# Up-projections of the gated MLPs as seven block products a tile, all seven low parts of its weights on GpSimd

## What is computed

```python
def conv_ffn(h, w_up, conv_w, conv_b, w_down):
    gate, val = jnp.split(h @ w_up, 2, axis=-1)
    gate = lax.conv_general_dilated(
        gate, conv_w[:, None, :], window_strides=(1,), padding=((CONV_WIDTH - 1, 0),),
        dimension_numbers=('NWC', 'WIO', 'NWC'), feature_group_count=D_FF) + conv_b
    return (jax.nn.silu(gate) * val) @ w_down

x = x + conv_ffn(rms_norm(x, ffn_norm_g[layer]), ...)      # D_FF = 2816, D_MODEL = 1024
```

## Time and profile before

| | |
|---|---|
| median of 3 runs | 1221.3 us |
| span of the profiled execution | 1219.5 us |
| up-projections in it, tiles 1 to 21 of a layer | 228.5 us, twice |
| down-projections in it, nine tiles of each | 97.9 us, twice |
| TensorE, VectorE, ScalarE, GpSimd busy | 1207.9, 507.8, 501.6, 567.4 us |
| granted TensorE clock, mean | 0.999 |

### The profile page before, as it was taken

The page is one execution under the profiler, slowest core; times in us unless marked ns, Lnnn a source line. Parts: engine busy times, 40 slices in busy tenths (PEclk is TensorE's granted clock), DMA queues, the critical chain, the costliest instruction groups (busy, mean ns, idle before and its releaser), DMA issues.

```text
span 1219.5 us, 16989 instructions
## 1 busy us (share of the span) xinstructions
PE 1207.9 (99%) x6230; PEld 1036.3 (85%) x6230; DVE 507.8 (42%) x900; ACT 501.6 (41%) x743; POOL 567.4 (47%) x509
## 2 busy tenths in 40 slices
PE   8999999999999999999999999999999999999997
PEld 7999999888888888888888889888888888888886
DVE  7878777653211212323241375635321212232325
ACT  6665555544322223423342366344332322343234
POOL 2435544335444444566645332613544444456662
PEclk9999999999999999999999999999999999999999
DMA  7222222113222222222223211301322222222221
GB/s 270 92 98 95 79 70 70 67 38 121 103 103 103 73 99 103 104 84 89 104 87 121 87 70 57 117 36 39 123 98 103 103 92 86 97 103 104 75 98 70
DMA packets 17325, 113.71 MB, mean 93 GB/s; under 512 B 1920, under 2 KB 2304, under 8 KB 4608
## 3 DMA queue, kind: packets, MB, share of 16 engines
q1 hardware_dynamic: 16416, 110.20, 25.2%
q10 hardware_dynamic: 864, 2.88, 0.7%
HBM read 110.98 MB, written 2.10 MB: 93 GB/s over the span
## 4 chain that ended last, share of the span: by engine, by line
PE 95%; DVE 2%; ACT 1%; issue 1%; DMA 0%; DVEq 0%; SPq 0%; ACTq 0%
PE ps L1600 38%; PE ps L1893 16%; PE ps L1681 9%; PE ps L1543 7%; PE ps L1572 3%; PE ps L2024 2%; PE ps L1722 2%; PE ps L1645 2%; PE ps L2004 2%; PE ps L1590 2%; PE ps L1650 1%; PE ps L1928 1%; PE ps L1708 1%; PE ps L1491 1%; PE ps L1734 1%
## 5 line engine op out<-in xcount | busy, mean ns | idle before, releaser
L316 POOL TENSOR_TENSOR w_lo<-w_raw,w_hi 128x512 fp32r<-128x512 f32 (+1 forms) x329 | 462.5, 1437 | 515.5 <-ACT w_hi L413 459.5
L413 ACT ACTIVATE w_hi<-w_raw 128x2048 fp32r<-128x2048 f32 (+1 forms) x93 | 171.9, 1848 | 309.1 <-PE ps L1600 155.2
L1600 PE MATMUL ps<-hT_hi,w_hi 128*128 128x512 f32 x688 | 267.7, 389 | 0.0
L1600 PE MATMUL ps<-hT_hi,w_lo 128*128 128x512 f32 x688 | 267.7, 389 | 0.0
L1600 PE MATMUL ps<-hT_lo,w_hi 128*128 128x512 f32 x688 | 267.6, 389 | 0.0
L1600 PEld LDWEIGHTS ps<-hT_hi,w_hi 128*128 128x128 f32 x688 | 129.1, 188 | 26.8
L1600 PEld LDWEIGHTS ps<-hT_lo,w_hi 128*128 128x128 f32 x688 | 129.1, 188 | 26.8
L1600 PEld LDWEIGHTS ps<-hT_hi,w_lo 128*128 128x128 f32 x688 | 129.1, 188 | 26.7
L1235 DVE TENSOR_TENSOR hT_lo<-region,hT_hi 128x2048 fp32r<-128x2048 f32 (+1 forms) x22 | 58.9, 2684 | 144.0 <-ACT hT_hi L686 144.0
L1205 DVE SCALAR_TENSOR_TENSOR qk<-ps,vec,qk 128x511 f32<-128x511 f32 x44 | 33.0, 750 | 200.1 <-ACT qk L660 200.1
L660 ACT ACTIVATE qk<-ps,vec 128x512 f32<-128x512 f32 x44 | 34.3, 780 | 175.5 <-PE ps L1600 166.3
(11 more groups left out here) (278 smaller groups left out, 2102.3 us busy)
## 6 DMA issues: line engine op xcount, KB each, us to landing
w_raw<-weights SPq DMA_DIRECT2D x99, 1024.0 KB, 4.8
gain<-gains ACTq DMA_DIRECT2D x4, 512.0 KB, 3.5
x<-x_in SPq DMA_DIRECT2D x3, 512.0 KB, 7.5
out<-region SPq DMA_DIRECT2D x3, 512.0 KB, 2.7
w_raw<-weights SPq DMA_DIRECT2D x2, 384.0 KB, 5.6
w_raw<-weights SPq DMA_DIRECT2D x1, 768.0 KB, 8.6
cst<-consts SPq DMA_DIRECT2D x1, 640.0 KB, 10.2
x<-x_in ACTq DMA_DIRECT2D x1, 512.0 KB, 4.1
```

What stands on the lines that cost most here:

```text
L316: ins = pool.tensor_tensor(w_lo[:, slot, cols], w_raw[:, slot, cols], w_hi[:, slot, cols].bitcast(f32), ALU.subtract)
L413: sc.activation(w_hi[:, slot, 0:used], w_raw[:, slot, 0:used], ACT.Copy).then_inc(w_hi_ready, 1)
L1600: ins = pe.matmul(bank, w[:, slot, k * pitch + 128 * s:k * pitch + 128 * s + 128], h[:, k:k + 1, :], start=k == 0 and n == 0, stop=k == KT ...
```

## The change

In both MLPs, up tiles 2 to 21 are no longer multiplied as 2 x 2 blocks in the plain way (eight block products) but as seven block products by Winograd's form of Strassen's scheme. The weights of a tile are four blocks A11, A12, A21, A22 (128 output channels by 512 inputs), the activations four blocks B11 to B22 (512 inputs by 256 tokens).

- **Weights.** VectorE makes S1 = A21 + A22, S2 = S1 - A11, S3 = A11 - A21 and S4 = A12 - S2 for each tile, 512 columns each (`block_sums`). ScalarE makes high parts of A11, A12, A22 in one instruction of 1536 columns, of S1 in one of 512, of S2 to S4 in one of 1536. GpSimd makes the seven low parts, 512 columns each (`block_lows`), where it made four.
- **Activations.** Once a layer, ScalarE copies the turned activations from PSUM to SBUF (`copy_raw`, eight instructions), and VectorE makes T1 to T4 and, with ScalarE, their two parts. T3 takes the place of B12.
- **Products.** Seven for each tile, each 4 input blocks x 3 products of 256 columns: 84 of 256 columns a tile (`block_tile`), in the order 1, 2, 3, 5, 6, 4, 7. Gate tiles use PSUM banks 0 to 3, value tiles 4 to 7.
- **Combining.** ScalarE copies product 1 to SBUF (`copy_p1`), VectorE combines the seven products in four instructions into `z` in SBUF (`combine_block`). The convolution's steps and the multiply by the SiLU read `z` instead of PSUM.
- **Edges.** The first two tiles of a layer are multiplied as before, in other banks. The first down tile reads `hT_hi`, `hT_lo` instead of `first_hi`, `first_lo`. `load_gain` moves from before the MLP to behind it.

```diff
+        T_PLACES = ((xn_at, xn_at + 4096), (xn_at + 8192, cst_at + 4 * C_CMUL), (act_end, act_end + 4096))
+        t_hi = [at(f"t_hi{j}", [128, 4, 256], a) for j, (a, b) in enumerate(T_PLACES)]
+        t_lo = [at(f"t_lo{j}", [128, 4, 256], b) for j, (a, b) in enumerate(T_PLACES)]
+        t_raw = [at(f"t_raw{j}", [128, 4, 256], b, f32) for j, (a, b) in enumerate(T_PLACES)]
+        z = region[:, 13312:15104]
+        p1 = (region[:, 15104:15360], vec[:, 0:256])
+        S_PLACES = ((region_at + 4 * 15360, late_at), (late_at + 4 * 1536, spare_at))
+        s_hi = [at(f"s_hi{j}", [128, 1536], a) for j, (a, b) in enumerate(S_PLACES)]
+        s_lo = [at(f"s_lo{j}", [128, 1536], b) for j, (a, b) in enumerate(S_PLACES)]
+        s_raw = [at(f"s_raw{j}", [128, 1536], b, f32) for j, (a, b) in enumerate(S_PLACES)]
+        s1_raw = [at(f"s1_raw{j}", [128, 512], w_lo_at + 4 * (UNIT * j + 1536), f32) for j in range(2)]
+        raw_h = region[:, 14 * SEQ:FT * SEQ].rearrange("p (j n) -> p j n", j=KT)
+        t3_raw = region[:, 12 * SEQ:14 * SEQ].rearrange("p (k n) -> p k n", k=4)
+        z1, z2 = z[:, 512:1024], z[:, 0:512]
...
+            def block_lows(l, n0):
+
+                with pool.Fori(1, PAIRS) as i:
+                    for half in range(2):
+                        tile = 2 * i + (half - 2)
+                        pool.wait_ge(w_hi_ready, 2 * i + (n0 + half + 1))
+                        for a in (0, 512):
+                            low(w_lo[:, half, a:a + 512], w_raw[:, half, a:a + 512], w_hi[:, half, a:a + 512])
+                        pool.wait_ge(s_summed[l], tile + 1)
+                        low(w_lo[:, half, 1024:1536], w_raw[:, half, 1024:1536], w_hi[:, half, 1024:1536])\
+                          .then_inc(w_lo_ready, 1)
+                        pool.wait_ge(s_high[l], 2 * tile + 1)
+                        low(w_lo[:, half, 1536:UNIT], s1_raw[half][:, :], w_hi[:, half, 1536:UNIT]).then_inc(s_low[l], 1)
+                        pool.wait_ge(s_high[l], 2 * tile + 2)
+                        for a, made in ((1024, s4_low[l]), (0, s_low[l]), (512, s_low[l])):
+                            low(s_lo[half][:, a:a + 512], s_raw[half][:, a:a + 512], s_hi[half][:, a:a + 512])\
+                              .then_inc(made, 1)
+
             pool.wait_ge(w_lo_ready, W_OUT0 + 1)
-            split_range(W_OUT0 + 1, W_C + 2)
+            split_range(W_OUT0 + 1, W_UP0 + 2)
+            block_lows(0, W_UP0)
+            split_range(W_DN0, W_C + 2)
...
+            def copy_raw(l, t, before):
+
+                for g in range(2):
+                    sc.wait_ge(turn_lo, 8 * before + 2 * t + g + 1)
+                    sc.activation(raw_h[:, 4 * g:4 * g + 4, t * 128:(t + 1) * 128],
+                                  ps[:, MLP_TURN[t] + g, :].rearrange("p (j n) -> p j n", j=4), ACT.Copy)\
+                      .then_inc(raw_copied[l], 1)
...
+                before_mlp = k in (1, 3)
+                if before_mlp:
+                    copy_raw(k // 2, 0, turns[0])
...
+                if before_mlp:
+                    for t in (2, 1, 3):
+                        copy_raw(k // 2, t, turns[0] - 1)
...
+                def block_high(i, half):
+
+                    sc.wait_ge(mm_done, 8 * i + 4 * (n0 + half - 1))
+                    sc.wait_ge(w_loaded[half], 16 * i + 16 * (n0 // 2 + 1))
+                    sc.activation(w_hi[:, half, 0:1536], w_raw[:, half, 0:1536], ACT.Copy).then_inc(w_hi_ready, 1)
+
+                def sum_highs(i, half):
+
+                    sc.wait_ge(s_summed[l], 2 * i + (half - 1))
+                    sc.activation(w_hi[:, half, 1536:UNIT], s1_raw[half][:, :], ACT.Copy).then_inc(s_high[l], 1)
+                    sc.activation(s_hi[half][:, :], s_raw[half][:, :], ACT.Copy).then_inc(s_high[l], 1)
+
+                def copy_p1(i, half):
+
+                    sc.wait_ge(product_done[l], 4 * i + (2 * half - 3))
+                    sc.activation(p1[half], ps[:, 4 * half + 3, 0:256], ACT.Copy).then_inc(p1_copied[l], 1)
...
+                    sc.wait_ge(act_done[l], 2)
+                    sc.wait_ge(product_done[l], 4 * LAST)
...
+                def pair(i, last=False):
+                    block_high(i, 1)
+                    copy_p1(i, 0)
+                    sum_highs(i, 1)
+                    if last:
+                        split_after(n1 - 2)
+                    else:
+                        block_high(i + 1, 0)
+                    copy_p1(i, 1)
+                    if not last:
+                        sum_highs(i + 1, 0)
+                    sc.wait_ge(combined[l], 2 * i + 1)
+                    for s in range(2):
+                        gate_start(i, s, (z1, z2)[s])
+                    silu(i)
...
+                for j, summed in enumerate((1, 3, 4)):
+                    sc.wait_ge(t_summed[l], summed)
+                    sc.activation(t_hi[j][:, :, :], t_raw[j][:, :, :], ACT.Copy).then_inc(t_high[l], 1)
+                for s in range(2):
+                    sc.wait_ge(mm_done, 4 * n0 + 2 * s + 2)
+                    gate_start(0, s, ps[:, 6 + s, :])
+                block_high(1, 0)
+                sum_highs(1, 0)
+                silu(0)
+                sc.wait_ge(t_summed[l], 4)
+                sc.wait_ge(mm_done, 4 * (n0 + 2))
+                sc.activation(hT_hi[:, 0:4, 256:512], t3_raw, ACT.Copy).then_inc(t_high[l], 1)
...
+                def block_sums(i, half):
+
+                    a11, a12, a22, a21 = (w_raw[:, half, 512 * j:512 * j + 512] for j in range(4))
+                    s1, (s2, s3, s4) = s1_raw[half][:, :], (s_raw[half][:, 512 * j:512 * j + 512] for j in range(3))
+                    ve.wait_ge(mm_done, 8 * i + 4 * (n0 + half - 1))
+                    ve.wait_ge(w_loaded[half], 16 * i + 16 * (n0 // 2 + 1))
+                    first = own.mark(ve.tensor_tensor(s1, a21, a22, ALU.add))
+                    ve.tensor_tensor(s3, a11, a21, ALU.subtract)
+                    own.wait(first)
+                    own.link(ve.tensor_tensor(s2, s1, a11, ALU.subtract))
+                    ve.tensor_tensor(s4, a12, s2, ALU.subtract).then_inc(s_summed[l], 1)
+
...
+                def combine_block(i, half, last=False):
+
+                    b = 4 * half
+                    if not last:
+                        ve.wait_ge(product_done[l], 4 * i + (2 * half - 2))
+                    else:
+                        ve.wait_ge(mm_done, 4 * n1)
+                    ve.wait_ge(p1_copied[l], 2 * i + (half - 1))
+                    own.link(ve.tensor_tensor(z[:, 512:1536].rearrange("p (a n) -> p a n", a=2)[:, :, 0:256], two(b),
+                                              p1[half].unsqueeze(1).broadcast_to([128, 2, 256]), ALU.add))
+                    ve.wait_ge(mm_done, 8 * i + 4 * (n0 + half + 1))
+                    u34 = z[:, 1280:1792].rearrange("p (a n) -> p a n", a=2)
+                    own.link(ve.tensor_tensor(u34, two(b + 1),
+                                              z[:, 1024:1280].unsqueeze(1).broadcast_to([128, 2, 256]), ALU.add))
+                    ve.tensor_tensor(z[:, 0:1536].rearrange("p (a n) -> p a n", a=2)[:, :, 0:256], two(b + 2), u34, ALU.add)
+                    ve.tensor_tensor(z[:, 256:512], ps[:, b + 1, 256:512], z[:, 1280:1536], ALU.add)\
+                      .then_inc(combined[l], 1)
...
+                def pair(i, last=False):
+                    block_sums(i, 1)
+                    if not last:
+                        block_sums(i + 1, 0)
+                    combine_block(i, 0)
+                    convolve(i, (z1, z2))
+                    if last:
+                        first_lows()
+                    combine_block(i, 1, last)
...
+                ve.wait_ge(raw_copied[l], 8)
+                b11, b12, b21, b22 = (raw_h[:, 4 * k:4 * k + 4, 256 * t:256 * t + 256] for k in range(2) for t in range(2))
+                first = own.mark(ve.tensor_tensor(t_raw[0][:, :, :], b12, b11, ALU.subtract))
+                own.wait(first)
+                ve.sem_inc(t_summed[l], 1)
+                ve.tensor_tensor(t3_raw, b22, b12, ALU.subtract).then_inc(t_summed[l], 1)
+                own.link(ve.tensor_tensor(t_raw[1][:, :, :], b22, t_raw[0][:, :, :], ALU.subtract))
+                ve.sem_inc(t_summed[l], 1)
+                ve.tensor_tensor(t_raw[2][:, :, :], b21, t_raw[1][:, :, :], ALU.subtract).then_inc(t_summed[l], 1)
+                for j in range(3):
+                    ve.wait_ge(t_high[l], j + 1)
+                    ve.tensor_tensor(t_lo[j][:, :, :], t_raw[j][:, :, :], t_hi[j][:, :, :].bitcast(f32), ALU.subtract)\
+                      .then_inc(t_low[l], 1)
+                convolve(0, (ps[:, 6, :], ps[:, 7, :]))
+                block_sums(1, 0)
+                for s in range(2):
+                    ve.wait_ge(silu_ready[l], s + 1)
+                    ve.wait_ge(mm_done, 4 * (n0 + 1) + 2 * s + 2)
```

(81 more changed lines are left out.)

157 lines of the change are left out of this document (85 added, 72 removed).

## The result

The changed kernel takes **1290.2 us** (median of four runs, 1288.66 to 1290.34) against 1221.34 (1220.79 to 1221.42) in the same session: ratio 1.0562, 95% interval 1.0547 to 1.0577. The profiled execution's span is 1286.8 us, mean granted TensorE clock 0.969; it is the shortest of the four runs (1288.66), 1.5 us under the median. The prediction was 1291.

The account below looks back on a forecast made before the run. TensorE, busy 99%, bounds the old kernel; in the changed one VectorE's fixed order, taking turns with GpSimd, sets 24.9 us a pair. +35.1 us a layer gives 1219.5 + 70.2 + 1.8 = 1291.5, stated as 1291; range 1240 to 1325.

Parts of the forecast that it names:

- Turns: GpSimd's lows and VectorE steps with two SBUF inputs never overlap; a 512-column step costs GpSimd 0.45 us.
- rival 2: Convolution steps (scalar_tensor_tensor) take no turns at 512 columns: 3.3 us instead of 6.9, 1249 us in all; chance 9%.
- The walk: One steady pair in VectorE's written order, zero at the end of tile (i,1)'s sums: 24.9 us a pair.
- (a): VectorE's sums of tile (i+1,0), four turns against GpSimd's lows of (i,1): 0 to 5.8 us.
- (c): ScalarE's gate start, 0.78 us, after the first combine; lets the convolution begin at 9.55 us.
- (d): Four convolution turns of 1.70 us on VectorE, the first waiting for a low: to 16.4 us.
- (e): VectorE's combine of tile (i,1), to 19.05 us; TensorE has finished that tile at 12.6.
- (g): Two multiplies in turns to 22.3 us, first sum to 22.9, three more without GpSimd to 24.9.
- The floor of 23.8: Least time of a pair, GpSimd's 14 lows plus VectorE's 14 steps without overlap: 23.8 us, 1271 in all.
- Rival 3: Slower by more: further waits in the ring of sums, highs, lows, products, or TensorE's clock falling; above 1325 us, 8%.
- Rival 1: GpSimd and VectorE overlap, so TensorE's 20.16 us bounds a pair: 1191 us, or 1195 to 1218 in part; chance 9%.
- Rival 4: Weight transfer or ScalarE becomes the bound; ScalarE put at 10.7 of 24.9 us a pair; no chance worth a number.

Follow-up runs that it names:

- the third run: Changed kernel with the eight sums, four convolution steps and two multiplies of each pair replaced by VectorE steps with one SBUF input: 1190.1 us, ratio 0.9745.
- the second: Changed kernel with only the four convolution steps and two multiplies of each pair replaced by VectorE steps with one SBUF input: 1232.4 us, ratio 1.0091.

## Why the prediction was right

**TensorE's price.** 84 products at 0.120 = 10.08; the run with the undisturbed pace shows 20.07 a pair and the one above 9.99 us for 84. Right, to 1%.

**Turns.** A low beside such a step: 1.70 expected, 1.65 to 1.74 seen. A step held: 1.70 expected; 1.66 to 1.83 seen, and 1.54 to 1.56 for each second tap of the convolution. The convolution at 512 columns, for which no row of before existed, was put with the two inputs in SBUF: 1.77 and 1.56 against 0.75, so rival 2 is out, and the rule of the Trainium skill ("SBUF — State Buffer", section "Who interferes with whom") holds for it too; its other half, that one SBUF input makes no conflict, is shown by the 0.68 us of the steps with one input.

**The walk.** Zero at 358.66 in the timeline above. (a) sums of (i+1,0) to 5.7, put at 5.8. (b) combine to 8.2 (8.4). (c) convolution from 9.37 (9.55). (d) to 16.2 (16.4). (e) combine to 18.9 (19.05). (g) multiplies in turns to 22.1 (22.3), then four sums that take 0.60 each, as in the walk. From the last sum of (1,1) to that of (10,1), nine periods, the pair is 24.73 in layer 0 and 24.92 in layer 1, put at 24.9. The floor of 23.8 would have been 18 us short over the kernel: it is the fixed order of one engine that was to be walked, not the sum of the work.

**Edges.** The third low of tile (1,1), which follows its sums, starts at 309.4 (zero was put at 309.5). The last sums end at 531.9 (533.6), and the first down tile starts 16.2 later (16.5): 548.15 (550.1). So 33.2 and 34.3 us a layer for 35.1. In layer 0 the nine periods were put 1.5 us too long and the two edges 0.4; in layer 1 the periods came out as put and the end 0.8 shorter. Inside the start small errors cancelled by luck: the sums of T took 5.0 for 4.4 us, the convolution of pair 0 took 2.9 for 3.3. The profiled execution, from which these rows are, took 1288.7, so the sum of 1291.5 is 2.8 above it; that the median, 1290.2, is closer is the spread of the runs.

**What was off without moving the sum.** I wrote that the lows would average 1.6 to 1.7. My own walk lets four of the 14 steps run without a low beside them, and (10 x 0.45 + 14 x 1.247)/14 = 1.57; measured 1.54. I also wrote that TensorE would wait 4 to 5 us a pair; it waits 2.7, because its granted clock falls (below) and its busy time grows from 20.16 to 22.1. Rival 3 priced a tenth of the products at half clock at 40 us, as if the lost time were on the path. It mostly wasn't: of 24.7 us a pair TensorE needs 20.16, and the slowdown was paid out of its waits, but for two pairs in layer 1 (below).

**Rivals.** Rival 1 fell with the third run, which shows it as the world without turns. Rival 2 fell with the second. Rival 4 never stood: ScalarE is busy 71 of 173 us, and weights still land 4.8 us after their issue.

## What to carry to other kernels

Before work is moved onto GpSimd and VectorE because they look half idle, ask of each new instruction whether both its inputs lie in SBUF, and count it as time of both GpSimd and VectorE; then walk one period in the written order of the engine that closes the loop. Moving a step from one of the two to the other helped little here (1278.7 at best for 1290.2), since it brings turns along, and a step put behind one that waits for TensorE can cost more than the step (56 us in all here). An algebraic saving can be taken for as many tiles as the side engines can carry: half of them gave 1.3% here, all of them cost 5.6%.
